# Loading x after the first modulation chunk, splitting one pair of weight tiles, and putting VectorE's maxima and masks ahead of the weights' low parts

## The reference

```
shift, scale, gate = split(silu(c) @ ada_w[i] + ada_b[i], 3)
h = rms_norm(x, norm_g[i]) * (1 + scale) + shift
q, kc, vc, ks, vs, kw, vw, gl, z = split_cols(h @ w_in, ...)
...
p_cmp = masked_softmax(q . k_cmp * scale, m_cmp)    # 15 compressed keys
p_slc, p_win = masked_softmax(q . k * scale, ...)   # 256 keys, 16 heads, twice
o = gate0 * p_cmp v_cmp + gate1 * p_slc v_slc + gate2 * p_win v_win
x = x + gate * ((o * silu(z)) @ w_out)
```

## Time and profile before

| what | value |
|---|---|
| time, median of 3 | 924.41 us |
| the profiled execution's own time | 924.84 us |
| its span on the core | 923.0 us |
| TensorE busy | 891.8 us (97%) |
| VectorE busy | 568.1 us (62%) |
| ScalarE busy | 493.8 us (53%) |
| GpSimd busy | 174.2 us (19%) |
| mean granted TensorE clock | 0.996 |

### The profile page before, as it was taken

The page is one execution under the profiler, slowest core; times in us unless marked ns, Lnnn a source line. Parts: engine busy times, 40 slices in busy tenths (PEclk is TensorE's granted clock), DMA queues, the critical chain, the costliest instruction groups (busy, mean ns, idle before and its releaser), DMA issues.

```text
span 923.0 us, 13041 instructions
## 1 busy us (share of the span) xinstructions
PE 891.8 (97%) x5005; PEld 765.1 (83%) x5005; DVE 568.1 (62%) x920; ACT 493.8 (53%) x780; POOL 174.2 (19%) x189
## 2 busy tenths in 40 slices
PE   2899999999999999999999999999999999999998
PEld 2788898998689988888888888898889888888886
DVE  5784777646877477555555547595557655555552
ACT  3544766645658456544444447686664654444431
POOL 1026355554064511000000004270000000000000
PEclk9999999999999999999999999999999999999999
DMA  9966655455572555655556556553334655555650
GB/s 362 330 208 205 206 183 166 132 160 178 165 247 75 194 172 165 204 189 189 183 185 186 161 152 194 154 166 93 92 116 138 205 182 182 183 185 184 210 173 23
DMA packets 45836, 163.26 MB, mean 177 GB/s; under 512 B 5200, under 2 KB 5584, under 8 KB 45776
## 3 DMA queue, kind: packets, MB, share of 16 engines
q1 hardware_dynamic: 45776, 162.44, 54.9%
HBM read 161.37 MB, written 1.05 MB: 176 GB/s over the span
## 4 chain that ended last, share of the span: by engine, by line
PE 86%; DVE 5%; ACT 4%; DMA 2%; issue 2%; POOL 1%; SPq 0%; ACTq 0%; DVEq 0%; POOLq 0%
PE bank L491 57%; PE bank L501 11%; PE bank L516 4%; DMA w_raw<-in_weights 2%; PE bank L664 2%; DVE w_lo L1637 1%; PE bank L868 1%; PE bank L670 1%; ACT w_hi L1094 1%; PE bank L747 1%; PE bank L690 1%; PE bank L692 1%; PE bank L691 1%; PE bank L596 1%; PE bank L695 1%
## 5 line engine op out<-in xcount | busy, mean ns | idle before, releaser
L1094 ACT ACTIVATE w_hi<-w_raw 128x1024 fp32r<-128x1024 f32 (+2 forms) x249 | 258.7, 1047 | 175.5 <-PE bank L491 152.1
L1637 DVE TENSOR_TENSOR w_lo<-w_raw,w_hi 128x1024 fp32r<-128x1024 f32 (+2 forms) x249 | 302.1, 1230 | 79.9 <-ACT w_hi L1094 79.2
L491 PE MATMUL bank<-w_hi,h_hi 128*128 128x512 f32 (+1 forms) x560 | 222.3, 397 | 3.0 <-DVE w_lo L1637 1.6
L491 PE MATMUL bank<-w_lo,h_hi 128*128 128x512 f32 (+1 forms) x560 | 218.2, 390 | 0.0
L491 PE MATMUL bank<-w_hi,h_lo 128*128 128x512 f32 (+1 forms) x560 | 172.8, 390 | 0.5 <-DVE h_lo L1666 0.5
L491 PEld LDWEIGHTS bank<-w_hi,h_hi 128*128 128x128 f32 x560 | 105.8, 189 | 25.2 <-issue 3.6
L491 PEld LDWEIGHTS bank<-w_hi,h_lo 128*128 128x128 f32 x560 | 105.5, 189 | 22.9 <-DVE h_lo L1666 1.1
L491 PEld LDWEIGHTS bank<-w_lo,h_hi 128*128 128x128 f32 x560 | 105.9, 189 | 20.0
L2460 POOL TENSOR_TENSOR ada_acc<-ada_acc,w_raw 128x512 f32<-128x512 f32 x56 | 79.4, 1418 | 81.3 <-ACT w_raw L1098 76.0
L501 PE MATMUL bank<-h_hi,w_hi 128*128 128x256 f32 x264 | 77.8, 295 | 0.2 <-ACT tok_k L1098 0.2
L501 PE MATMUL bank<-h_lo,w_hi 128*128 128x256 f32 x264 | 75.3, 285 | 0.0
(11 more groups left out here) (315 smaller groups left out, 1383.5 us busy)
## 6 DMA issues: line engine op xcount, KB each, us to landing
w_raw<-in_weights SPq DMA_DIRECT2D x298, 512.0 KB, 4.4
w_raw<-in_weights SPq DMA_DIRECT2D x4, 360.0 KB, 3.5
x<-in_x SPq DMA_DIRECT2D x1, 1024.0 KB, 8.1
gate_row<-in_gate_bias SPq DMA_DIRECT2D x2, 512.0 KB, 7.0
out<-x SPq DMA_DIRECT2D x4, 256.0 KB, 3.1
w_raw<-in_weights SPq DMA_DIRECT2D x3, 256.0 KB, 2.7
const<-in_constants SPq DMA_DIRECT2D x1, 285.5 KB, 5.1
cols<-in_columns SPq DMA_DIRECT2D x1, 208.5 KB, 2.5
```

Of the source, the lines that this page charges most:

```text
L491: mm = e.matmul(pb[t][:, 0:n], xs, (wh, wl)[p][:, kk * n:(kk + 1) * n], start=(k + kk == 0 and q == 0 and p == 0), stop=(k + kk == kts - 1 ...
L1094: e.activation(w_hi[i % NSPLIT][:, 0:c], raw[v % NRAW][:, 0:c], ACT.Copy).then_inc(*rounded(v))
L1637: e.tensor_tensor(w_lo[i % NSPLIT][:, 0:c], raw[v % NRAW][:, 0:c], w_hi[i % NSPLIT][:, 0:c].bitcast(F32), ALU.subtract).then_inc(*rested(v))
```

## The change

There are four edits.

1. SP loads all four units of `ada0_0` before x; the identity follows x. On VectorE the products of unit 4 come before `norm_means(0)`.
2. `ada_columns(3)` on TensorE is issued between the two token halves of unit 1 of kskw, no longer behind both.
3. Filling 9 moves from bank 6 to bank 4, and the first compressed scores wait for the maximum of filling 7, no longer 9.
4. On VectorE, in z0 and z1, `rests` of a unit comes behind the maxima (and, in the first two units of z1, behind the compressed scores' masks and shift); the masks of the compressed scores come before the two maxima. Only the first `rests` of z0 stays where it was.

```
-                bank = ... order[n % 4] if s == "moba" or n < 8 else 6 if n == 9 else (7, 4)[n % 2] if n < 18 else 2 + n % 2
+                bank = ... order[n % 4] if s == "moba" or n < 8 else (7, 4)[n % 2] if n < 18 else 2 + n % 2
...
                         mm.then_inc(*streamed((u, t)))
+                        if between and t == 0:
+                            between(j)
...
+            def last_columns(j):
+                if j == 1:
+                    ada_columns(3, banks[5], spread.at((0, 1)))
+
+            kskw = linear("nsa_kskw", 1, (h_hi, h_lo), h_first, True, [ada_cols.at(2)], late=h_late,
+                          between=last_columns)
...
             ada_columns(1, banks[4], spread.at((0, 0)))
             steps_of(kskw, 1)
-            ada_columns(3, banks[5], spread.at((0, 1)))
...
                     compressed_scores(j, (banks[5], banks[6]),
-                                      (c_masked.at(0) if j else m_reduced.at(("nsa", 9)),))
+                                      (c_masked.at(0) if j else m_reduced.at(("nsa", 7)),))
...
             mac_chunk(0)
+            mac_chunk(2, 0)
             norm_means(0)
-            mac_chunk(2, 0, 1, 2)
+            mac_chunk(2, 1, 2)
...
             for j, u in enumerate(of["nsa_z0"]):
-                rests(u, 4)
                 if j == 0:
+                    rests(u, 4)
                     q_rests("nsa_q1", "nsa_q", 1, banks[7])
                 maxima("nsa", 3 * j, 3 * j + 1, 3 * j + 2)
+                rests(u, 4)
             for j, u in enumerate(of["nsa_z1"]):
-                rests(u, 4)
                 if j == 0:
                     z_products("nsa_z0", 0, 0, 0)
                     z_products("nsa_z0", 0, 0, 1)
+                if j < 2:
+                    compressed_masks(j)
                 if j < 3:
                     maxima("nsa", 12 + 2 * j, 13 + 2 * j)
                 if j < 2:
                     compressed_shift(j)
+                rests(u, 4)
...
             e.dma_start(cols[:, :], cols_d).then_inc(*cols_in())
-            fetch(0)
-            fetch(1)
+            for u in range(of["ada0_2"][0]):
+                fetch(u)
             e.dma_start(x[:, :, :], ...).then_inc(*x_in())
-            fetch(2)
             e.dma_start(const[:, 0:2 * P], const_d[:, 0:2 * P]).then_inc(*eye_in())
-            for u in range(3, of["nsa_kcvc"][2]):
+            for u in range(of["ada0_2"][0], of["nsa_kcvc"][2]):
                 fetch(u)
```

More of the change, by code:

```diff
@@ L408, in program @@
                 h0, nh, wd = n // 3 * per + (n % 3 == 2) * (per // 2), per // (1 + t), P * (1 + t)
-                bank = (4, 6, 5, 7)[n % 4] if s == "moba" and n > 7 else order[n % 4] if s == "moba" or n < 8 else 6 if n == 9 else (7, 4)[n % 2] if n < 18 else 2 + n % 2
+                bank = (4, 6, 5, 7)[n % 4] if s == "moba" and n > 7 else order[n % 4] if s == "moba" or n < 8 else (7, 4)[n % 2] if n < 18 else 2 + n % 2
                 fillings[s].append(dict(
@@ L469, in tensor, with linear @@
             w = Lane(e)
-            def linear(name, pair, lhs, ready, tokens_out, free, k0=0, late=lambda k: []):
+            def linear(name, pair, lhs, ready, tokens_out, free, k0=0, late=lambda k: [], between=None):
                 hi, lo = lhs
@@ L761, in tensor @@
             kcvc = linear("nsa_kcvc", 0, (h_hi, h_lo), h_first, True, [ada_cols.at(0)], late=h_late)
-            kskw = linear("nsa_kskw", 1, (h_hi, h_lo), h_first, True, [ada_cols.at(2)], late=h_late)
+            def last_columns(j):
[3 more added lines that the diff above has]
+                          between=last_columns)
             steps_of(kcvc, 2)
@@ L2024, in vector, with compressed_masks @@
                                     1.0, 0.5, ALU.add, ALU.mult).then_inc(*gates_done())
-            def compressed_shift(tt):
+            def compressed_masks(tt):
                 sv = by_head(scr[:, tt, 0:512], CPAD)
@@ L2043, in compressed_shift @@
                             step(last)
+            def compressed_shift(tt):
+                sv = by_head(scr[:, tt, 0:512], CPAD)
                 w.wait_ge(*c_masked.at(tt))
```

## The result

The changed kernel takes 926.07 us, the median of 22 runs (924.15 to 928.35), where the kernel before takes 923.81 us in 22 runs beside them (922.60 to 925.78). The ratio is 1.0025 with a 95% interval of 1.0019 to 1.003: 2.3 us slower, between 1.8 and 2.8 us.

A forecast was written before the change was run, and what follows sets the result against it. TensorE, busy nearly all the time, was taken as the bound, so only its waits and clock count. 924.84 - 0.2 - 1.4 + 3.2 = 926.4 us, with half of possible delays 926.6 us; range 923.2 to 928.4 us.

The forecast's parts named there:

- the wait that it named: z1: a new TensorE wait for `w_lo` of 2 to 3 us at about 143 us, before the third unit.
- The base: Whole kernel: the sum starts at the profiled execution, 924.84 us, 0.43 us over a median of 924.41 us.
- Load order: Start: unit 4's products ready earlier, `norm_means` now inside that chain; 0.2 us gain, between -0.5 and +0.4 us.
- Columns: 35 to 48 us: `h_hi` and `w_lo` come 1.44 us earlier; gain 1.4 us, between 1.0 and 1.6.
- The bank: About 130 us: filling 11 waits up to 0.6 us for filling 9's maximum; counted as nothing, covered by a later wait.
- VectorE's order: z1: third unit's low part stalls TensorE 2.3 us, fourth's is 3.2 us late, between 0 and 4.1 us.
- filling 11's share: About 130 us: half of filling 11's and the load chain's possible delay (up to 0.6 us), raising 926.4 to 926.6 us.
- GpSimd's share: z1: beside GpSimd's six sums the subtraction takes 1.67 us, a low part 2.30 us, against 0.69 and 1.23 us.
- (a): z1: VectorE keeps pace between GpSimd's sums, edit 4 costs 0 to 0.3 us; 923.4 us; chance 0.17.
- (b): z1: VectorE keeps pace and the half clock goes too, 1.57 us more; 921.9 us; chance 0.15.
- (c): z1: TensorE's stall brings the half clock onto the fourth unit too, 1.57 us more; 928.2 us; chance 0.13.
- (d): Start: x comes late enough to hold `norm_means`, 0.5 us on top; 927.1 us; chance 0.05.

The follow-up runs named there:

- the maxima ahead of the masks: Changed kernel with each unit's low parts made first again in z0 and z1, and maxima again before masks: 922.36 us, ratio 0.9984.
- the masks first: Also "the rests first": changed kernel with low parts made first again in z0 and z1, masks still before maxima: 923.97 us, ratio 1.0004.
- short sums: GpSimd's sums over modulation chunk 5 cut from 512 columns to one: changed kernel 923.48 us (0.9993), kernel before 922.42 us (0.9989).
- the third unit's rests first: Changed kernel with the rests of z1's third unit first again, the fourth's left behind maxima and masks: 925.84 us, ratio 1.0026.
- the best order: Edits 1 and 2, old banks and z0, z1 reordered (first unit: rests, maxima, masks, products, shift; later: maxima, rests, masks, shift): 921.30 us, ratio 0.9975.
- the rests between: Changed kernel with z1's rests moved up between the masks and the maxima: 925.27 us, ratio 1.0016.

## Why the prediction was right, point by point

It forecast 926.6 us, from 923.2 to 928.4, with slower the likeliest; the median is 926.07 us, and the wait that it named is the one that came.

**The base.** The sum began at the profiled execution, 924.84 us; 22 runs put the kernel before at 923.81 us. That is 1.0 us too high. The forecast change was +1.8 us (926.6 - 924.84), the measured +2.3 us (1.8 to 2.8). Part of the closeness of 926.6 to 926.07 us is these two errors against each other.

**Load order: -0.2 us forecast, 0.0 measured** (-0.8 to +0.8 us by its ratio). The loads kept the forecast's distance: x is there 1.64 us ahead of unit 4 (12.03 and 13.67 us, forecast 12.8 and 14.4 us). What was mis-sized are unit 4's two products, 4.04 / 5 x 2 = 1.6 us in the sum and 1.27 us in the trace (13.67 to 14.94 us); the first is a TENSOR_SCALAR of 0.49 us. So `norm_means` finds the squares not done, waits 0.21 us, and the 0.2 us of gain is spent there.

**Columns: -1.4 us forecast, -0.9 and -1.2 us measured** in two kernels. The mechanism is as told: `h_hi` came 1.38 us earlier beyond the start's shift. The wait at 43 us fell from 1.65 to 0.15 us. What is late next, the fourth unit of kcvc, moved too, from 47.93 to 45.76 us, 1.37 us beyond the start's 0.80; there TensorE waits 1.18 us for ScalarE's rounding of its weights, which the half clock hid in the kernel before. The medians gain 0.9 and 1.2 us, at the low end of the forecast's 1.0 to 1.6. That fits the two profiles in which a late weight unit left 0.6 us of the gain, and the waits in z1 that took some of it back; how often each happens, the timed runs don't tell.

**The bank: counted at nothing.** Filling 11 waits 0.4 us in the trace of after, of the 0.6 us at most. Where a low part stands in front of that maximum, the wait is longer than the forecast's 0.6 us: 1.17 us with the maxima ahead of the masks and 1.36 us with the masks first. Even so the time doesn't show it. The kernel with the first two edits and the one with the maxima ahead of the masks do the same in the same order but for the bank, and they stand at 0.9987 and 0.9984: -0.3 us, between -1.5 and 0.9 us.

**VectorE's order: +3.2 us forecast, and 0.2 us with filling 11's share; the bank and the order measured +4.2 us alone (3.1 to 5.5), and +3.5 us on top of the first two edits** (1.0025 - 0.9987 = 0.0038). From the first two edits alone it splits by one kernel after the other: with the shared bank and the split of masks and shift -0.3 us (0.9987 to 0.9984, which is nothing), with the masks ahead of the maxima +1.8 us (to 1.0004), with the low parts behind, in z0 and z1, +1.9 us (to 1.0025). In the prediction the lateness was all the low parts', and the masks were even credited with removing a wait of 0.6 us. It did see that fillings 14 and 15 wait for the maxima, and gave that no price. So this term has the right size with half of its cause missing, which is luck; the split holds for one sequence of kernels, and the masks' place with the low parts left behind was not run. The prediction also put the masks right behind the products, at 136.98 us, with ScalarE's first tanh as late as in the earlier trace rows. With VectorE's order alone that was so (137.28 us, no idle time). In the kernel after the products began at 132.16 us, 4.2 us earlier than in the earlier trace rows, and VectorE idled 1.22 us before the masks. The columns' edit accounts for 1.4 us of this at most, and 0.6 us is the low part that no longer stands in front of the products (136.39 against 135.78 us, the end of the first tanh); the rest is a load. Ahead of the tanh ScalarE rounds a weight unit, and this is when it came, in the kernel before and after:

```profile
134.16 1.06 ACT L1094 ACTIVATE w_hi<-w_raw 128x1024 fp32r<-128x1024 f32 x1 [3.82 <-DMA w_raw<-in_weights]
130.44 1.06 ACT L1101 ACTIVATE w_hi<-w_raw 128x1024 fp32r<-128x1024 f32 x1 [2.19 <-DMA w_raw<-in_weights]
```

Over the fourteen profiles it came between 130.35 and 134.37 us, at 132.19 us with the load order alone and at 132.37 us with the first two edits. Of the six profiles with the masks ahead of the maxima, right behind the products, VectorE idled before them in four (0.48 to 1.22 us) and not in two. So how much the change loses by it goes by the execution, and the early load is also the main reason why the third low part was ready at 141.65 us where the prediction had 144.77 us.

**GpSimd's share.** The prediction gave the subtraction 1.67 us and each low part 2.30 us. Measured with VectorE's order alone: 0.69, 2.29 and 2.30 us, and 0.43 to 0.62 us for the bound, counted at 0.21. The difference between 144.77 and 144.1 us is mostly the subtraction's. With short sums the loss of the change falls from 2.3 us to 0.4 us (0.9993 against 0.9989; -0.8 to 1.5 us). That is the net loss. If the first two edits still gain their 1.2 us, the bank and the new order still cost some 1.6 us with short sums, of 3.5 us (an estimate from these ratios): the long sums make about half of it.

**Rivals.** (a) and (b), that VectorE keeps pace between the sums, are excluded by the wait of 1.7 us and by the median. (c), the half clock on the fourth unit too, isn't in the profile of after, but is in that with the third unit's rests first, where the chain's 4.36 us for the fourth unit is 1.5 us over 2.87 us and the rest of the span comes out at 776.4 us in place of 774.6 us from its start. The Trainium skill, TensorE: Matmul & The Clock Gate, section What's actually happening, has the throttled clock as the default that activity releases. This case agrees for the waits of 1.7 and 2.3 us, with a granted clock of 0.50 soon behind them; and where z1 has no wait at all, in the best order, the clock stays at 1.00. But with the rests between, waits of 1.61 and 1.01 us in z1 left it at 1.00 from 138 to 152 us, and the kernel before had 0.50 there too with no wait for `w_lo`. So a wait of this length doesn't decide the clock, and the change didn't bring the lower one. (d), x late for `norm_means`, is there in kind and not in size: 0.21 us of waiting in place of 0.5 us, enough to take the load order's gain.

**What stays open.** The second chunk's columns begin anywhere between 19.94 and 21.32 us in the same code because the first square does between 11.83 and 13.20 us, when x has landed; why the loads land at different times, here and at 130 us, was not tried. How much of the masks' 1.8 us is VectorE's idle time before the masks and how much the late maxima was not separated.

## What to carry to other kernels

Before a step is moved ahead on an engine, see in the timeline whether its input is already there at its new place: work put in front of a wait hides it, work put behind it lengthens the chain. Where an engine prepares operands for TensorE's next units, every such operand has its own slack, and one late operand is enough: making only the first early moved the wait of 1.7 us to the next one, where it was 2.3 us. Where an effect of 0.2% is asked for, compare a late event in the trace less an early one, and timed runs, not two spans; and look whether a stretch at the lower clock or a late load lies between the two events. Where a load is moved, check each input of the step behind it: here a step with 0.2 us to spare in the plan had 0.2 us too little.

## What the runs showed of the hardware that was not expected

- VectorE's operations on SBUF beside GpSimd's sums. A low part (two SBUF inputs) takes 1.22 us beside sums of one column and mostly 2.2 to 2.3 us beside sums of 512 columns; but amid such sums it also took 1.41 and 1.68 us (the rests between) and 1.21 us (the best order), so it isn't held each time. The sums stretch as well: six took 9.68 us, where one alone took 1.28 us. The Trainium skill, SBUF — State Buffer, section SBUF: two separate sides, says that VectorE with two SBUF inputs and a GpSimd operation that reads SBUF exclude each other, the first to start holding the ports to its end; the lengths agree, since 2.29 us is 1.07 us more than 1.22 us, and that is less than one sum of 1.28 us.
- A tiny operation can be held as long as a large one. The bound on 128x16 elements took 0.18 us with short sums, 0.56 and 0.61 us in the kernel after, and 1.24 us in the one with the maxima ahead of the masks:

```profile
138.35 1.24 DVE L2059 TENSOR_SCALAR stats<-stats 128x16 f32<-128x16 f32 x1
```

It isn't held always: in the kernel before it took 0.18 us at 141.20 us, amid long sums, and the subtraction behind it took 1.67 us in place of 0.69 us. Where the bound was held (1.14 to 1.24 us in four profiles), the subtraction kept its 0.69 us. The reductions beside it kept 0.67 to 0.69 us in every one of these kernels. The Trainium skill, SBUF — State Buffer, section SBUF: two separate sides, has VectorE's operations with two SBUF inputs, and those in a mode that uses the second pair of ports, as the ones that the lock holds; that a scalar operation of this shape runs in such a mode is not shown by any run here.

- A stretch at 1.2 GHz need not cost anything. Here are the kernel before (granted clock 0.50) and the one with the load order alone (1.00) in the same stretch:

```profile
46.00:47.00 1.00, 1.00 (x4) 0.71 (x3) 0.82 (x2) 1.00 (x2) 0.00 (x0) 0.50 1.01 414
```

```profile
46.00:47.00 1.00, 0.00 (x0) 0.01 (x1) 1.00 (x2) 1.00 (x2) 0.00 (x0) 1.00 1.03 422
```

At a clock of 0.50 TensorE is busy where at 1.00 it stands idle, 1.18 us in all, until ScalarE has rounded the next weights; the fourth unit of kcvc begins in both when they are ready, at 47.93 and 47.02 us, which is the 0.90 us by which their columns differ (20.95 and 20.05 us). In the kernel after, the 14 runs with a mean granted clock of 0.998 have a median of 925.9 us and the two at 1.000 one of 925.8 us. But the five at 0.996 have one of 926.9 us, and of the 33 runs of the kernel before beside the one with the rests first, nine at 1.000 have a median of 923.9 us, 19 at 0.998 one of 924.0 us, and five at 0.996 one of 925.2 us. More of the lower clock does cost about 1 us.
